# A fused two-block transformer kernel: the second feed-forward's up projection as seven block products in chunks two to four

## What is computed

```python
D_MODEL, SEQ = 1024, 512
D_FF_2 = 4 * D_MODEL
...
        h = rms_norm(x, norm_mlp[l])
        x = x + jnp.square(jax.nn.relu(h @ w_up[l])) @ w_down[l]
    return rms_norm(x, norm_final)
```

## Time and profile before

| | us |
|---|---|
| median of 3 runs | 1462.06 |
| lowest, highest run | 1461.99, 1462.33 |
| the profiled execution, its own time | 1462.24 |
| span of that execution in the profile | 1460.5 |
| busy in the span: TensorE | 1450.5 (99%) |
| VectorE | 1028.1 (70%) |
| ScalarE | 664.6 (46%) |
| GpSimd | 20.0 (1%) |

### The profile page before, as it was taken

One profiled execution on the slowest core, in us unless ns is written; L12 is line 12 of the kernel. 1 busy time (PEld: TensorE's weight loads), 2 busy tenths in 40 slices (PEclk: granted clock), 3 DMA queues, 4 the chain that ended last, 5 costly groups with the idle time before them and its releaser, 6 DMA issues.

```text
span 1460.5 us, 20058 instructions
## 1 busy us (share of the span) xinstructions
PE 1450.5 (99%) x7500; PEld 1217.7 (83%) x7500; DVE 1028.1 (70%) x1590; ACT 664.6 (46%) x954; POOL 20.0 (1%) x21
## 2 busy tenths in 40 slices
PE   9999999999999999999999999999999999999998
PEld 7878788888889888988988888888888888888886
DVE  6837774676678577767967887956656585857668
ACT  6214554324434334334734655525444644545354
POOL 0000000000000000000000000000000000000000
PEclk9999999999999999999999999999999999999999
DMA  6623222223531531430232323224215333150401
GB/s 233 238 87 101 79 79 87 87 87 111 206 87 35 182 91 40 135 97 29 87 116 87 128 88 119 73 66 123 72 30 160 143 119 113 41 175 15 173 0 58
DMA packets 38850, 148.93 MB, mean 102 GB/s; under 512 B 4168, under 2 KB 4680, under 8 KB 35572
## 3 DMA queue, kind: packets, MB, share of 16 engines
q1 hardware_dynamic: 34656, 137.90, 29.2%
q10 hardware_dynamic: 4116, 9.96, 2.0%
HBM read 145.72 MB, written 6.06 MB: 104 GB/s over the span
## 4 chain that ended last, share of the span: by engine, by line
PE 97%; DVE 1%; DMA 1%; issue 0%; ACT 0%; POOLq 0%; ACTq 0%; POOL 0%; SPq 0%
PE ps L1472 31%; PE ps L1473 30%; PE ps L1474 30%; PE ps L1623 1%; PE ps L1636 1%; PE ps L2832 1%; PE ps L1513 0%; DMA stage<-stream_dram 0%; DVE y L2551 0%; DMA wgu<-wgu_dram 0%; PE ps L1506 0%; PE ps L2852 0%; PE ps L2990 0%; PE ps L2864 0%; PE ps L1681 0%
## 5 line engine op out<-in xcount | busy, mean ns | idle before, releaser
L1472 PE MATMUL ps<-hh,wh 128*128 128x512 f32 x1088 | 430.7, 396 | 0.1
L1474 PE MATMUL ps<-hh,wl 128*128 128x512 f32 x1088 | 424.0, 390 | 0.0
L1473 PE MATMUL ps<-hl,wh 128*128 128x512 f32 x1088 | 423.8, 390 | 0.0
L689 ACT ACTIVATE wh<-stage 128x1024 fp32r<-128x1024 f32 x130 | 137.1, 1057 | 235.2 <-PE ps L1474 230.3
L1472 PEld LDWEIGHTS ps<-hh,wh 128*128 128x128 f32 x1088 | 204.4, 188 | 46.3 <-issue 4.3
L1474 PEld LDWEIGHTS ps<-hh,wl 128*128 128x128 f32 x1088 | 204.2, 188 | 43.4
L1473 PEld LDWEIGHTS ps<-hl,wh 128*128 128x128 f32 x1088 | 204.5, 188 | 39.5
L983 DVE TENSOR_TENSOR wl<-stage,wh 128x1024 fp32r<-128x1024 f32 x129 | 157.3, 1221 | 45.5 <-ACT wh L689 45.2
L2517 DVE TENSOR_TENSOR wl<-raw,wh 128x1024 fp32r<-128x1024 f32 x56 | 67.7, 1220 | 37.4 <-ACT wh L2035 37.4
L2035 ACT ACTIVATE wh<-raw 128x1024 fp32r<-128x1024 f32 x56 | 59.4, 1060 | 73.4 <-PE ps L1474 73.3
L1474 PE MATMUL ps<-xch,wl 128*128 128x256 f32 x308 | 87.2, 283 | 0.0
(11 more groups left out here) (373 smaller groups left out, 2627.2 us busy)
## 6 DMA issues: line engine op xcount, KB each, us to landing
stage<-stream_dram SPq DMA_DIRECT2D x198, 512.0 KB, 3.7
raw<-down_dram SPq DMA_DIRECT2D x24, 1024.0 KB, 6.7
bias_lines<-bias_line ACTq DMA_DIRECT2D x1, 3840.0 KB
raw<-down_dram SPq DMA_DIRECT2D x4, 768.0 KB, 5.2
bias<-bias_lines ACTq DMA_DIRECT2D x4, 512.0 KB, 4.9
out_dram<-scaled SPq DMA_DIRECT2D x4, 512.0 KB, 3.0
x<-x_dram SPq DMA_DIRECT2D x3, 512.0 KB, 7.2
bias<-bias_lines ACTq DMA_DIRECT2D x4, 256.0 KB, 2.9
```

The source lines that it names most:

```text
L689: A(parts_of(b, p)[0], b.stage[:, p.stage, :], ACT.Copy).then_inc(s.hi_ready, 1)
L1472: MM(out, wh, xh, start=start, stop=False, skip_group_check=True)
L1473: MM(out, wh, xl, start=False, stop=False, skip_group_check=True)
L1474: return MM(out, wl, xh, start=False, stop=stop, skip_group_check=True)
```

## The change

The first chunk keeps its eight up panels. In chunks two to four the up stretch is made by the seven-product scheme too: the weight of a chunk is cut in two groups g of 512 hidden columns, and each group is seven blocks `Block2(c, g, product)` in the order P1, Q5, P6, P2, P7, Q3, R4. A block is 512 inputs by 256 hidden columns: 4 x 2 x 3 matmuls with a 128x128 weight piece held and 256 tokens moving. Four combinations of h are new: `xsh` and `xsl`, high and low parts of four sums of x's quarters, made in the first chunk from x scaled by `norm_mlp` (ScalarE `scale_x`, eight; VectorE `x_sums`, four; then `x_sums_hi` and `x_sums_rest`, four each, during the first chunk's down stretch). x is turned earlier for that, after and within panels 0 to 2, since the sums are made in place of x.

After a block is done: ScalarE copies P1's bank (`block_seed`) and the banks of Q5 and P6 (`block_copy`), VectorE subtracts for P7 and Q3 (`block_take`), ScalarE takes relu and square, and the combinations for the down stretch are made for two pairs at a time (`block_singles_hi`, `block_sums`, `block_sums_hi`, `block_singles_rest`, `block_sums_rest`).

The sums of weights are divided: each of the three sums that the seven products need starts as a transfer. `raw_sum` gets quarter 0 by a plain transfer from SP (`base`), and GpSimd issues a transfer that adds quarter 1 to it (`add_first`); quarter 2 is added to quarter 1 in `raw` by another adding transfer (`add_third`). VectorE adds the other two (`second_sum`, `fourth_sum`), two for each group and half. This holds for the blocks and, in chunks two to four, for the units too. All transfers of these chunks are 512 KB. The kernel before issues no transfer from GpSimd.

```diff
@@ sync_program @@
+    def base(c, h, unit):
+        sp.dma_start(b.raw_sum[:, h, :], weights(c, h, unit, 0)).then_inc(s.base_in[h].sem, 16)
+
+    def block(c, h, unit, r):
+        sp.dma_start(b.raw[:, r, h, :], weights(c, h, unit, r)).then_inc(s.block_in[h][r].sem, 16)
...
+        if c < CHUNKS2 - 1:
+            for h in range(2):
+                sp.wait_ge(s.lo_ready, Unit2(c, P1A + 2 * h).index + 1)
+                block(c + 1, h, False, 0)
+            for h in range(2):
+                sp.wait_ge(s.summed.sem, s.summed.at(summed_by(Unit2(c, R4A + h), R4)))
+                base(c + 1, h, False)
+            for r, j in ((1, P7A), (2, Q3A), (3, R4A)):
+                for h in range(2):
+                    sp.wait_ge(s.lo_ready, Unit2(c, j + h).index + 1)
+                    block(c + 1, h, False, r)
@@ gpsimd_program @@
+    def add_first(c, h, unit):
+        lap = 2 * (c - 1) + unit
+        pool.wait_ge(s.base_in[h].sem, s.base_in[h].at(16 * lap + 16))
+        if lap:
+            pool.wait_ge(s.added_in[h], 32 * lap)
+        G.dma_start(b.raw_sum[:, h, :], weights(c, h, unit, 1), accum_op=ALU.add).then_inc(s.added_in[h], 16)
+
+    def add_third(c, h, unit):
+        lap = 2 * (c - 1) + unit
+        pool.wait_ge(s.block_in[h][1].sem, s.block_in[h][1].at(16 * lap + 16))
+        pool.wait_ge(s.added_in[h], 32 * lap + 16)
+        G.dma_start(b.raw[:, 1, h, :], weights(c, h, unit, 2), accum_op=ALU.add).then_inc(s.added_in[h], 16)
+
+    for c in range(1, CHUNKS2):
+        add_first(c, 0, False)
+        add_first(c, 1, False)
+        add_third(c, 0, False)
+        add_third(c, 1, False)
+        for h in range(2):
+            add_first(c, h, True)
+            add_third(c, h, True)
@@ scalar_program, chunks two to four @@
+            block_seed(at(P1))
+            block_hi(at(P7))
+            if before:
+                block_sums_hi(before, 0)
+            block_copy(at(Q5), BANK_D[g], 0)
+            block_hi(at(Q3))
+            block_copy(at(P6), BANK_B[g], 1)
...
+            block_hi(following[0])
+            rectify_bank(at(P2), BANK_A[g], 1, 1)
+            block_hi(following[1])
+            rectify_taken(at(P7), 2, 1)
+            block_hi(following[2])
+            rectify_taken(at(Q3), 3, 2)
+            rectify_bank(at(R4), BANK_B[g], 0, 2)
+            block_singles_hi(at(R4))
@@ vector_program, chunks two to four @@
+            block_lo(at(R4))
+            block_lo(following[0])
+            block_take(at(P7), 1)
+            block_lo(following[1])
+            second_sum(following[1])
+            block_take(at(Q3), 2)
+            block_lo(following[2])
+        last = Block2(c, 1, R4)
+        block_sums(last, 0)
+        block_singles_rest(last)
+        block_sums_rest(last, 0)
@@ tensor_program @@
-    def up(c, u):
+    def up(u, turned=None):
...
+            if turned and k == 5:
+                turn_x(turned)
...
+    def block(c, g, product, opens=False):
+
+        p = Block2(c, g, product)
+        pe.wait_ge(s.lo_ready, p.index + 1)
+        bank = {P2: BANK_A, Q5: BANK_D, Q3: BANK_D}.get(product, BANK_B)[g]
+        for m in range(PAIRS2):
+            high, low = x_block(product, m)
+            for n in range(2):
+                at = M * m + P * n
+                ins = three(b.ps[:, bank, M * n:M * n + M], b.wh[:, p.slot, at:at + P], b.wl[:, p.slot, at:at + P],
+                            high, low, opens and m == 0 and n == 0, m == PAIRS2 - 1)
+        ins.then_inc(s.panel_done, 1)
...
+                pe.wait_ge(s.block_copied.sem, s.block_copied.at(3 * n + 1))
+                block(c, g, P6)
+                block(c, g, P2)
+                pe.wait_ge(s.block_copied.sem, s.block_copied.at(3 * n + 3))
+                block(c, g, P7)
```

More of the change, by code:

```diff
@@ L634, in sync_program, with up_row @@
         load_row(row, row + UNITS1 - RING)
[L636 to L647 removed]
+    def up_row(u):
+        p = Up2(u)
+        sp.wait_ge(s.lo_ready, p.index - RING + 1)
+        sp.dma_start(b.stage[:, p.stage, :], stream[P_FF2 - UNITS1 + u]).then_inc(s.load[p.stage], 16)
@@ L1460, in gpsimd_program, with weights @@
     power(4)
+    def weights(c, h, unit, r):
+        return dram["down2"][c, r, :, h, :] if unit else dram["up2"][c - 1, h, r]
+    def add_first(c, h, unit):
[14 more added lines that the diff above has]
+        add_third(c, 1, False)
+        for h in range(2):
+            add_first(c, h, True)
+            add_third(c, h, True)
     for n, part in enumerate((slice(2, 4), slice(0, 1), slice(1, 2))):
@@ new lines, in block_sums_hi @@
+    def block_sums_hi(p, first):
+        act.wait_ge(s.combined.sem, s.combined.at(PAIRS2 + 2 * p.number + 1 + first))
+        sums = x_quarters((b.spare1, b.spare2)[first][:])[:, :, 0, 0, :].rearrange("p (b n) c -> p n b c", n=2)
+        A(b.xch[:, 2 * p.half:2 * p.half + 2, 3 + first:7:2, :], sums, ACT.Copy).then_inc(s.act2_hi, 1)
+    for u in range(KT):
+        if u == 0:
+            copy_x(0)
+        elif u == 1:
+            copy_x(1)
+            copy_x(2)
+        elif u == 2:
+            copy_x(3)
+        if u < RING:
+            up_hi(Up2(u + RING))
+        elif u < KT - 1:
+            unit_hi(Unit2(0, u - RING))
+        square(u)
+        if u == KT - 1:
+            unit_hi(Unit2(0, u - RING))
+        if u % 2:
+            combination_hi(u // 2)
+        if u == 2:
+            for k in range(KT):
+                scale_x(k)
@@ new lines, in by_pair, with pairs_of, block_singles_rest @@
+    def by_pair(ap):
+        return ap.rearrange("p b n c -> p n b c")
+    def pairs_of(p):
+        return slice(2 * p.half, 2 * p.half + 2)
+    def block_singles_rest(p):
+        dve.wait_ge(s.act2_hi, 2 * PAIRS2 + 3 * p.number + 1)
+        V.tensor_tensor(b.xcl[:, pairs_of(p), 0:3, :], by_pair(b.block[:, 1:4, :, :]),
+                        f32(b.xch[:, pairs_of(p), 0:3, :]), ALU.subtract).then_inc(s.act2_ready, 1)
+    sums1, sums2 = (x_quarters(part[:])[:, :, 0, 0, :] for part in (b.spare1, b.spare2))
@@ new lines, in block2_vector @@
+    raw_sum(0, 2, 1, 4)
+    unit_lo(Unit2(0, P6A))
+    unit_lo(Unit2(0, P6B))
+    unit_lo(Unit2(0, P2A))
+    raw_sum(1, 2, 0, 5)
+    unit_lo(Unit2(0, P2B))
+    raw_sum(1, 2, 1, 6)
+    unit_lo(Unit2(0, P7A))
+    raw_sum(3, 0, 0, 7)
+    dve.wait_ge(s.x_copied.sem, s.x_copied.at(TT))
+    take(0, 1, P6B, early, right, 0, b.nr2)
+    unit_lo(Unit2(0, P7B))
+    raw_sum(3, 0, 1, 8)
+    take(0, 2, Q5B, late, right, 4, b.r2)
+    unit_lo(Unit2(0, Q3A))
+    x_sums_rest(0)
+    unit_lo(Unit2(0, Q3B))
```

494 lines of the change are left out of this document (348 added, 146 removed).

## The result

The changed kernel takes **1452.26 us** (median of 6 runs, 1452.06 to 1452.98) against 1462.16 us (1461.62 to 1462.42) for the kernel before in the same comparison. The ratio is 0.9933, with a 95% interval of 0.9921 to 0.9946. So it is faster by 9.9 us, or 0.7%, more than the 2.9 us taken as "no change". The forecast was 1452.7 with a range of 1451.6 to 1460.0.

What follows compares the result with a forecast made beforehand. TensorE's matmuls and new gaps between them were taken as the bound. Profiled execution 1462.24 - 9.6 (matmuls) + 0.2 (tightest place) = 1452.8, or 1452.7 against the median, other terms 0; range 1451.6 to 1460 us.

Steps and rivals of the forecast that it cites:

- TensorE's term: Chunks two to four: 576 matmuls of 512 columns removed (130.5 us), 1008 of 256 added (121.0 us), net -9.6 us.
- rival 3: In the blocks, the weight load sets the pace of 256-column matmuls, 193.5 instead of 121.0 us: 1525 us; chance 0.02.
- Turning x: First chunk: same 32 transposes, waits for ScalarE's bank copies just fit, cost 0 (0.5 us each for two if not).
- First chunk: New scalings and sums on ScalarE and VectorE there are hidden, backlog of 3 us worked off: 0, bounded by 1 us.
- rival 4: First chunk's new work or new waits are not hidden, 2 to 9 us of the saving go: 1457 us; chance 0.06.
- ScalarE and VectorE in later chunks: Chunks two to four: ScalarE busy 50, VectorE 66 of 78.4 us; both fit, VectorE nearly full in second groups.
- The tightest place: End of a chunk's second group, VectorE's take of Q3 to TensorE's P1B: room 0.3 us, t the end of block Q3.
- The 0.2 us taken in the sum: Allowance for waits at the tightest place of each chunk, 0.2 us in all, with 0 to 3 for the range.
- Rival 1: VectorE's full stretch slips or GpSimd's issuing holds it back: 3 to 4 us, 1456 us, still faster; chance 0.17.
- Transfers: GpSimd's adding transfers land after 7 us (bounds 3.7 and 14.4), no gap while the landing L is under 13 us.
- The chain's budget: From one chunk's units to the next's blocks, two landings in a row must take less than 26.2 us.
- rival 2: Adding transfers are late, from a landing of L = 13 us; at 15 us +20, so 1472.7 us; chance 0.14.

Runs made afterwards that it cites:

- x8_turn: The changed kernel with x turned after each of panels 0 to 3 of the first chunk, scalings and sums one panel later: 1456.83 us.
- x4_extra1: The changed kernel with three small linked VectorE instructions ahead of the take of Q3 in each chunk's second group: 1454.59 us.
- x1_wide: The changed kernel with each block as 12 matmuls of 512 columns instead of 24 of 256, output not the reference's: 1448.88 us.
- x7_dve: The changed kernel with first and third additions made by VectorE from plain transfers, GpSimd issuing nothing: 1458.38 us.
- x5_extra2: The changed kernel with seven small linked VectorE instructions ahead of the take of Q3 in each chunk's second group: 1458.32 us.
- x6_plain: The changed kernel with GpSimd's 24 transfers plain instead of adding, output not the reference's: 1452.19 us in one run.
- x10_wide_order: x1_wide with VectorE's take of P7 moved ahead of the next block's low part, in both groups of a chunk: 1451.10 us.

## Why the prediction was right, point by point

**TensorE's term** (-9.6): right to 0.1 us. The blocks' matmuls follow each other at 0.120 us and a chunk takes 78.42 and 78.40 us, where 78.4 was worked out from the earlier trace rows. The weight load sets no other pace (rival 3): it is busy in all 19.90 us of a window of blocks, but does not lengthen it. That is against the Trainium skill, "TensorE: Matmul & The Clock Gate", "Back-to-back issue gap", by whose figures this term was estimated at +23 us. This form of matmul has 0.120 and 0.227 us for 256 and 512 columns in the trace, and the measurement decides.

**Turning x** (0): right as placed, with 0.08 us at each of the four groups. But the zero was argued from the bank's copies alone. x8_turn shows that one panel later costs 4.6 us, by the work queued behind it.

**First chunk** (hidden, bounded by 1 us): right, -0.11 us measured. "Hidden" had 0.9 us of room before P1A, which the prediction did not work out; it spoke of a backlog worked off. So the zero is in part luck, and rival 4 was nearer than its 0.06 says.

**ScalarE and VectorE in later chunks:** 50 and 66 of 78.4 us predicted; measured 49.8 and 67.4 in the second chunk, 48.9 and 65.8 in the third. The dense group was put at 18 of 20.2; a window of 19.90 us in it has 17.80.

**The tightest place:** found and sized. Predicted take at t + 2.3, rest at t + 8.0, wanted at t + 8.3, room 0.3. Measured t + 2.2, t + 7.8, t + 8.35, and a room of 0.38 us by x4_extra1. The next tightest, the take of P7 before R4, was given 0.6 us: it ends at 1244.52 and R4 starts at 1245.21, 0.69 later. x1_wide and x7_dve waited there as well. The 0.2 us taken in the sum did not come. Rival 1 did not come either, and GpSimd's issuing held nothing back: VectorE's instructions last 1.22 us beside it as in the earlier trace rows. x4_extra1, x5_extra2 and x7_dve show that it would have been real.

**Transfers:** the weakest term, and right in its sign. A landing of 7 us was assumed; it was 8.0 in the median and 9.5 in the chain that matters. The chain's budget was put at 26.2 us for two landings, and the trace has 1294.7 - 1268.4 = 26.3. The room was 26.2 - 14 = 12.2 by the prediction and is 26.3 - 19.0 = 7.3 us. By that budget it decides from L = 13 as said, so rival 2 was 3.5 us of landing away and not 6. The plain transfer of GpSimd's path, for which the prediction had worked out 3.2 us, took 6.0 in the median of x6_plain. What the prediction left out is GpSimd's own order, through which a delay in its issuing counts three times. It is also why the chain from blocks to units is not of the same form, as the prediction had it, though its room is about as large (7.4 us).

**Sum:** 1452.7 against 1452.26. Of the 0.4 between them 0.2 is the unused term. The rest is within what the runs scatter, of which the start of the feed-forward alone has 0.5 us between the two profiles.

## What to carry to other kernels

Price a fast multiplication scheme by the distance between matmuls in a row at the new size, since here an eighth fewer products at half the length gave 7% of the stretch and not 12.5%. Then look for the place where the engines behind have the least room, with the take, the combination and the unit that wants it on one time line: an average of 66 of 78 us hid a place with 0.38 us, and one more panel of delay in the first chunk costs 4.6 us. Before moving an instruction forward, look at what it will wait for in every place where the edit puts it (x10_wide_order). Additions of weights can be given to adding transfers where a chain of some 20 us for two of them fits. GpSimd worked its list in order here, so a late entry holds up the other half's too; no run tested another order of the list.
